# Decoder layer on one core: weight place 4 turned round and filled earlier, last expert tile's rows added in PSUM

## Chip, cores and metric

One NeuronCore of one Trainium2 chip. The metric is the device time of one execution in microseconds (us). Times on the profile's axis count from the first instruction of the profiled execution.

## What is computed

One hybrid decoder layer over 1024 tokens of 1024 float32 values: adaLN modulation, a projection, sparse attention (8 heads) beside differential attention (4 heads), an output projection, then a mixture of experts with 32 experts. The reference, cut to the part that the change touches:

```python
x = x + gate_a[:, None] * jnp.dot(o, w_out[l])
h = rms_norm(x, g_moe[l]) * (1.0 + scale_m[:, None]) + shift_m[:, None]
# hier_moe: top-1 group, top-2 experts in it, gates[token, expert]
y = jnp.zeros_like(h)
for e in range(N_EXPERTS):
    hid = jax.nn.silu(jnp.dot(h, w_gate[e])) * jnp.dot(h, w_up[e])
    y = y + gates[:, e:e + 1] * jnp.dot(hid, w_down[e])
x = x + gate_m[:, None] * y
return rms_norm(x, g_final)
```

## The kernel before

Each engine runs its own list of instructions, written out by hand, and they meet at semaphores. SyncE (SP) issues nearly all plain DMAs, GpSimd (POOL) the indirect ones. Tokens are taken in T = 8 tiles of P = 128.

**Projection loop** (lines 1900 to 1953 on TensorE, 1387 to 1422 on VectorE, 530 to 562 on SyncE). For tile t, TensorE multiplies the attention output in `HT[:, :, 128 t ...]` by `wo` (QKV columns 12288 to 20479, `project_out`, L1861) in two halves of 512 columns; VectorE scales by `gate_row` (QKV columns 22528 to 23551, L1410) and adds the residual into `XT[t]`. The result is stored to DRAM (`residual_rows` for the first 6 tiles, `h_rows` for all 8 normalised ones, `store_h2`), and routing (L1296 and after) chooses experts. It ends with `lst` (L1426), the list of the rows that each expert tile gathers.

**Expert stage.** The pairs of token and expert are packed into NSTEP = 20 expert tiles of 128 rows, numbered 0 to 19. For tile n TensorE runs `turn_rows` (L1963, transposes the gathered rows), `gate_up` (L1976), `turn_hidden` (L1985) and `down_proj` (L1999). ScalarE and VectorE evict between them (ScalarE `ev_t` L950, `ev_sg` L958, `ev_h` L964; VectorE `ev_hid` L1487 and L1489, `ev_y` L1497). POOL gathers the rows of `h_rows` (L690) and scatters each result tile to `expert_rows` in DRAM (`y_dram`, L697). The order on TensorE in a step is

```python
for n in range(NSTEP):
    turn_hidden(n, n % 2)
    if n + 1 < NSTEP: gate_up(n + 1, (n + 1) % 2, *weights_of(n + 1))
    if n + 2 < NSTEP: turn_rows(n + 2, n % 2, 16 * (n // 2 + 2))
    down_proj(n, n % 2, *weights_of(n))
```

**Weights.** An expert has 2 MB of gate and up (`gate_up_load`, L410, two DMAs of 1 MB) and 1 MB of down (`down_load`, L414). The 32 experts pass through RING = 6 places: 0, 1, 3 and 4 are quarters of QKV, 2 lies in X, and place 5 in SC and BIAS. An expert tile takes its rows from one to four experts. SyncE refills a place's gate and up part once the last `gate_up` that needs it is done (`gu_ps`), and its down part after the last `down_proj` (`dn_ps`). Experts 0 to 3 are loaded within or just after the projection loop, gate and up of place 4 after the last `project_out`, and its down part and place 5 only after routing has ended and the first two gathers have landed. `gate_row` lies in place 4's region.

**Tail.** After `down_proj(17)` the 6 spilled residual tiles are read back into `XT` (L572, "x2_back"). When all scatters have landed (`rows_out`), SyncE reads `expert_rows` back, 16 DMAs of 512 KB (L597), two to a token tile. TensorE sums tiles 0, 2, 4 and 6 (`mixed`) in PSUM (`add_into`, L2037): XT times the identity, and each of the two result tiles times a diagonal matrix with its routing weight. VectorE does tiles 1, 3, 5 and 7 (`combine`, L1540 and L1542). ScalarE then squares and sums each tile (L1000), POOL makes the reciprocal root (L635, L636), VectorE scales (`finish`, L1552) and SyncE stores the tile (L600).

## Time and profile before

| | us |
|---|---|
| median of 3 runs | 1051.61 (1050.21 to 1052.73) |
| the profiled execution, its own time | 1047.62 |
| its span, first to last instruction | 1045.8 |
| TensorE busy in the span | 952.2 (91%) |
| VectorE / ScalarE / GpSimd busy | 595.3 / 403.9 / 115.7 |
| mean granted TensorE clock | 0.973 of full |
| DMA: bytes moved | 191.44 MB |

A row's times come from the one profiled execution. "Busy" is the time with an instruction in flight; an idle time is put down to what ended it. The chain of waits goes back from the last instruction to what released each step. The granted clock is 1.00 at 2.4 GHz and 0.50 at 1.2 GHz. In the profile each float32 matmul of 512 columns appears as two records.

### The profile page before, as it was taken

Reading aid. Unit: us, or ns where it says so; the run is one execution under the profiler, and the core shown is the slowest. Engines: PE = TensorE matmul, PEld = TensorE weight load, DVE = VectorE, ACT = ScalarE, POOL = GpSimd, SP = SyncE. Lnnn points to the kernel's source line nnn. Section 1 sums busy time; section 2 is a strip of 40 time slices with the busy share of each in tenths; the row PEclk is TensorE's granted clock in tenths of the full one; section 3 lists DMA queues with packets and bytes.
Section 4 is the critical chain, followed back from the end, with each engine's and each line's share of the span. In section 5 each row is a group of like instructions: output and inputs, shape, how many; then the busy total and the mean of one; then the engine's idle time right before and its main releaser. Section 6 shows DMA issues by size and latency. Waiting matters only on the chain.

```text
span 1045.8 us, 14947 instructions
## 1 busy us (share of the span) xinstructions
PE 952.2 (91%) x5302; PEld 513.1 (49%) x5302; DVE 595.3 (57%) x1593; ACT 403.9 (39%) x909; POOL 115.7 (11%) x218
## 2 busy tenths in 40 slices
PE   3899999999999798879999899999499999979974
PEld 2463675444449476546666545556233434323421
DVE  3479548999997687777676333456333222312217
ACT  6130236666620577767668412122121111211113
POOL 3000000000038001110000000000111111111003
PEclk9999999999999999989999999999599999999989
DMA  9996101101111000040000411166899999999979
GB/s 326 331 359 228 41 22 41 41 21 40 40 30 18 1 1 1 1 173 11 1 2 2 161 61 60 61 261 248 323 418 422 419 417 422 419 421 421 397 284 377
DMA packets 69916, 191.44 MB, mean 183 GB/s; under 512 B 10248, under 2 KB 36160, under 8 KB 57552
## 3 DMA queue, kind: packets, MB, share of 16 engines
q1 hardware_dynamic: 61856, 172.63, 43.1%
q0 software_dynamic: 5760, 16.78, 4.1%
q10 hardware_dynamic: 2224, 1.05, 0.4%
q8 instruction: 43, 0.70, 0.3%
q14 instruction: 33, 0.27, 0.1%
HBM read 172.60 MB, written 22.04 MB: 186 GB/s over the span
## 4 chain that ended last, share of the span: by engine, by line
PE 79%; DMA 6%; issue 4%; DVE 4%; ACT 3%; SPq 3%; POOL 0%; POOLq 0%; ACTq 0%; DVEq 0%
PE PS L1675 16%; PE PS L1976 12%; PE PS L1861 11%; PE PS L1778 6%; PE PS L1999 6%; PE PS L1799 4%; PE PS L1821 3%; DMA SC<-in_w_up_dram 3%; PE PS L1722 3%; PE PS L1684 3%; PE PS L1816 3%; SPq L450 2%; PE PS L1963 2%; PE PS L1699 2%; PE PS L1664 1%
## 5 line engine op out<-in xcount | busy, mean ns | idle before, releaser
L1675 PE MATMUL PS<-HT,X 128*128 128x512 f32 x384 | 168.8, 593 | 0.0
L1976 PE MATMUL PS<-QKV,HT 128*32 128x512 f32 (+2 forms) x640 | 130.4, 607 | 3.4 <-DMA SC<-in_w_up_dram 1.7
L860 ACT ACTIVATE X<-X,nmx 128x896 f32<-128x896 f32 (+7 forms) x128 | 98.6, 772 | 68.5 <-DVE nmx L1205 68.0
L1675 PEld LDWEIGHTS PS<-HT,X 128*128 128x128 f32 x384 | 72.5, 190 | 92.4 <-issue 92.2
L1861 PE MATMUL PS<-QKV,HT 128*128 128x512 f32 x256 | 115.3, 604 | 0.0
L1141 DVE TENSOR_SCALAR_CACHE_REDUCE BIAS<-SC,tk 128x384 f32<-128x384 f32 (+3 forms) x128 | 96.4, 809 | 1.1
L1487 DVE TENSOR_TENSOR HT<-PS,HT 128x256 f32<-128x256 f32 x20 | 8.5, 425 | 153.3 <-ACT HT L958 153.3
L1778 PE MATMUL PS<-QKV 64*128 64x512 f32 (+3 forms) x384 | 82.1, 533 | 10.8 <-DVE nmx L1205 10.0
L837 ACT ACTIVATE X<-SC,tk 128x896 f32<-128x896 f32 x64 | 69.6, 1087 | 43.1 <-DVE tk L1129 43.1
L1861 PEld LDWEIGHTS PS<-QKV,HT 128*128 128x128 f32 x256 | 48.0, 193 | 54.6 <-issue 54.5
L1999 PE MATMUL PS<-QKV,HT 128*32 128x512 f32 (+2 forms) x320 | 65.4, 595 | 2.2 <-DMA X<-in_w_down_dram 2.2
L1205 DVE CUSTOM_DVE_ANT_0 X<-PS,R 128x256 f32<-128x256 f32 (+7 forms) x80 | 51.0, 675 | 28.6 <-PE PS L1778 28.2
L1799 PE MATMUL PS<-ident,X 128*128 128x128 f32 x432 | 66.1, 284 | 0.0
L1976 PE MATMUL PS<-SC,HT 128*32 128x512 f32 (+2 forms) x144 | 57.8, 604 | 6.3 <-issue 6.3
L958 ACT ACTIVATE HT<-PS 128x256 f32<-128x256 f32 x20 | 7.7, 384 | 143.3 <-PE PS L1976 143.3
L1976 PEld LDWEIGHTS PS<-QKV,HT 128*32 128x32 f32 (+2 forms) x640 | 38.1, 120 | 49.0 <-issue 46.2
L1976 PE MATMUL PS<-X,HT 128*32 128x512 f32 (+2 forms) x160 | 58.4, 621 | 0.8 <-DVE HT L1506 0.8
L1205 DVE CUSTOM_DVE_ANT_0 X<-PS,SC 128x1024 f32<-128x1024 f32 (+5 forms) x48 | 42.0, 887 | 29.4 <-PE PS L1778 29.4
L1799 PEld LDWEIGHTS PS<-ident,X 128*128 128x128 f32 x432 | 48.5, 143 | 10.6 <-issue 9.1
L1816 PE MATMUL PS<-QKV,HT 128*128 128x128 f32 x288 | 41.8, 291 | 11.1 <-ACT HT L870 11.0
L1778 PEld LDWEIGHTS PS<-QKV 64*128 64x128 f32 x384 | 32.5, 189 | 39.2 <-issue 25.2
L1821 PE MATMUL PS<-QKV 128*64 128x128 f32 x576 | 46.7, 285 | 4.1 <-ACT QKV L870 2.8
(295 smaller groups left out, 1462.9 us busy)
## 6 DMA issues: line engine op xcount, KB each, us to landing
QKV<-in_w_gate_dram SPq DMA_DIRECT2D x22, 1024.0 KB, 16.4
QKV<-in_w_up_dram SPq DMA_DIRECT2D x22, 1024.0 KB, 22.9
QKV<-in_w_down_dram SPq DMA_DIRECT2D x22, 1024.0 KB, 28.2
QKV<-in_w_ada_dram SPq DMA_DIRECT2D x8, 2048.0 KB, 15.5
QKV<-in_w_ada_dram SPq DMA_DIRECT2D x8, 1024.0 KB, 12.6
X<-in_w_in_dram SPq DMA_DIRECT2D x16, 512.0 KB, 3.8
QKV<-expert_rows SPq DMA_DIRECT2D x16, 512.0 KB, 10.0
X<-in_w_gate_dram SPq DMA_DIRECT2D x5, 1024.0 KB, 16.5
```

The costliest lines, as they stand in the source:

```text
L837: act.activation(RL[:, n % 2, 0:w], SC[:, sc_off[t]:sc_off[t] + w], ACT.Sign, bias=tk[:, 4, i:i + 1].bitcast(F32), scale=-1.0, accum_out=c ...
L860: act.activation(sc, sc, ACT.Exp, bias=nmx[:, i % 4, m:m + 1], scale=-1.0, accum_out=rs[:, i, m:m + 1]).then_inc(exp_done, 1)
L1141: dve.tensor_scalar(BIAS[:, i % 3, 0:w], SC[:, sc_off[t]:sc_off[t] + w], thr.bitcast(F32)[:, i:i + 1], 0.0, ALU.is_lt, ALU.add, accum_out= ...
L1205: dve.tensor_tensor_reduce(sc_buf[i % 4][:, m, 0:w], PS[:, 2 * m:2 * m + 2, :].rearrange("p a n -> p (a n)")[:, BANK * n:BANK * n + w], aw ...
L1675: end = pe.matmul(PS[:, 2 * b + half, :], WS[:, b, j, :], HT[:, j, BANK * half:BANK * (half + 1)], start=(j == 0), stop=(j == KC - 1))
L1778: end = pe.matmul(PS[:, 2 * m + n + c0 // BANK, 0:c1 - c0], QKV[rows_m, q0:q0 + P], QKV[rows_m, k0 + c0:k0 + c1], start=True, stop=True)
L1799: end = pe.transpose(PS[:, 4 + g % 2, c0:c0 + P], sc_buf[i % 4][:, m, P * b:P * (b + 1)], ident[:, :])
L1816: end = pe.matmul(PS[:, 6 + h % 2, slot], turned_at(i)[:, g % 4, P * (b - b0):P * (b - b0 + 1)], vf[:, u * S + P * b:u * S + P * (b + 1)], ...
L1821: end = pe.matmul(PS[DH * m:DH * (m + 1), 6 + h % 2, slot], vd[:, b, v0:v0 + DH], turned_at(i)[:, g % 4, c0:c0 + P], start=(b == 0), stop= ...
L1861: end = pe.matmul(PS[:, n % 4, :], HT[:, k, P * (n // 2):P * (n // 2 + 1)], wo[:, k, BANK * (n % 2):BANK * (n % 2 + 1)], start=(k == 0), s ...
L1976: end = pe.matmul(PS[at, 2 + b, :], hgT[b][:, P * c_ + at.start:P * c_ + at.stop], WGU[w][:, c_, :, :], start=(c_ == 0), stop=(c_ == KC - 1))
L1999: end = pe.matmul(PS[at, 5 + h, :], hidT[b][:, P * c_ + at.start:P * c_ + at.stop], WDN[w][:, c_, BANK * h:BANK * (h + 1)], start=(c_ == 0 ...
```

## The change

1. Place 4 is turned round: its down weights now lie in its first 2048 columns (over `wo`), its gate and up weights in the other 4096 (over `gate_row`). From token tile 4 on, the gate row is read from a second copy, `gate_late`, loaded into the columns of `HT` that `project_out` of tile 0 has used.
2. Gate and up of place 4 are loaded inside the projection loop, at t = 5. Gate and up of place 5 are loaded once all h2 stores have landed and the last router product is done, no longer after the gathers. Its down weights and those of place 4 still come after them.
3. The result tile 19 (LAST) is not scattered. VectorE multiplies it by its rows' routing weights (`w_row`, fetched from DRAM by an indirect DMA at n = 4, `ev_y_last`) and keeps it in `y_last`. A marking matrix `belongs` (128 rows by 1024 tokens, 0 or 1, `mark_last_rows`) says which token each row is of. TensorE adds `belongs` times `y_last` into all 8 token tiles. So that rows nobody scatters read as zero, 32 DMAs write zeros over `expert_rows` during the attention.
4. At the end the order on TensorE is `down_proj(18)` before `gate_up(19)`. The read-back of token tiles 0 to 2 starts once scatter 18 has landed, that of tiles 3 to 7 also waits for `down_proj(19)`.
5. All 8 token tiles are begun in PSUM (`begin`), in two rounds of four pairs of banks; tiles 4 to 7 wait until a pair is free again.

```diff
-        gu_at = [a[:, 0:4096] for a in homes] + [SC[:, 0:4096]]
-        dn_at = [a[:, 4096:6144] for a in homes] + [BIAS[:, 0:2, :].rearrange("p a n -> p (a n)")]
+        gu_at = [a[:, 0:4096] for a in homes[0:4]] + [homes[4][:, 2048:6144], SC[:, 0:4096]]
+        dn_at = [a[:, 4096:6144] for a in homes[0:4]] + [homes[4][:, 0:2048], BIAS[:, 0:2, :].rearrange("p a n -> p (a n)")]
...
+            for r in range(2 * T):
+                for h in range(2):
+                    sp.dma_start(y_dram[P * r:P * (r + 1), BANK * h:BANK * (h + 1)],
+                                 wuk[:, :, :].rearrange("p h d -> p (h d)")).then_inc(small_in, 16)
...
             for t in range(SPILLED):
-                if t == EARLY + 1:
+                if t == 1:
+                    sp.wait_ge(op_ps, 2)
+                    sp.dma_start(gate_late, mod_dram[:, 0:D].partition_broadcast(P).rearrange(
+                        "p o (k n) -> p (o k) n", k=KC)).then_inc(out_row_in, 16)
+                elif t == EARLY + 1:
                     for w in range(IN_X):
                         gate_up_load(sp, expert_of(w), w)
                         down_load(sp, expert_of(w), w)
+                    sp.wait_ge(op_sb, 2 * EARLY)
+                    gate_up_load(sp, expert_of(RING - 2), RING - 2)
...
+            for i in range(2):
+                sp.wait_ge(h2_out[i], 16 * (T // 2))
+            sp.wait_ge(lg_ps, T)
+            gate_up_load(sp, expert_of(RING - 1), RING - 1)
+            sp.wait_ge(route_done, 1)
+            for i in range(2):
+                sp.wait_ge(xg_in[i], 16)
...
             sp.wait_ge(rows_out, 1)
             for t in range(T):
+                if t == 3:
+                    sp.wait_ge(dn_ps, 2 * NSTEP)
                 for k in range(2):
...
+            def ev_y_last():
+                dve.wait_ge(w_in, 16)
+                for h in range(2):
+                    part = slice(BANK * h, BANK * (h + 1))
+                    dve.wait_ge(dn_ps, 2 * LAST + h + 1)
+                    dve.scalar_tensor_tensor(out=y_last[:, part], in0=PS[:, 5 + h, :], scalar=w_row, in1=out_row[:, part],
+                                             op0=ALU.mult, op1=ALU.mult).then_inc(y_sb, 1)
...
+                if n == LAST - 1:
+                    down_proj(n, n % 2, *weights_of(n))
                 if n + 1 < NSTEP:
                     gate_up(n + 1, (n + 1) % 2, *weights_of(n + 1))
                 if n + 2 < NSTEP:
                     turn_rows(n + 2, n % 2, 16 * (n // 2 + 2))
-                down_proj(n, n % 2, *weights_of(n))
+                if n != LAST - 1:
+                    down_proj(n, n % 2, *weights_of(n))
...
+            def begin(t):
+                add_into(t, ident[:, :], XT[:, t, :], True, False)
+                end = add_into(t, belongs[:, P * t:P * (t + 1)], y_last, False, t not in mixed)
+                if t not in mixed:
+                    end.then_inc(mix_ps, 1)
+            def mix(t):
+                i = mixed.index(t)
+                pe.wait_ge(yg_in[t], 32)
+                add_into(t, diag[:, i, 0, :], yg[t][0], False, False)
+                add_into(t, diag[:, i, 1, :], yg[t][1], False, True).then_inc(mix_ps, 1)
             pe.wait_ge(x2_back, 16 * SPILLED)
+            pe.wait_ge(y_sb, 2 * NSTEP)
+            pe.wait_ge(diag_done, 9)
+            pe.wait_ge(rows_out, 1)
+            for t in range(4):
+                begin(t)
+            mix(0)
+            mix(2)
+            pe.wait_ge(fin_done, 1)
+            begin(4)
+            pe.wait_ge(cb_done, 1)
+            begin(5)
+            mix(4)
+            pe.wait_ge(fin_done, 3)
+            begin(6)
+            pe.wait_ge(cb_done, 2)
+            begin(7)
+            mix(6)
```

TensorE at the tail, before (L2037 is the matmul of `add_into`; the rows ahead of it close the branch for overflow tiles):

```order
L2024 REGISTER_ALU
L2024 COMPARE_AND_BRANCH
L2021 UNCONDITIONAL_BRANCH
L2037 MATMUL PS<-X,ident 128x512 x8
L2037 MATMUL PS<-QKV 128x512 x16
L146 UNCONDITIONAL_BRANCH
```

and now, the first twelve groups of four or more (L2112 is the same line of the changed file):

```order
L2112 MATMUL PS<-X,ident 128x512 x2
L2112 MATMUL PS<-QKV 128x512 x2
L2112 MATMUL PS<-X,ident 128x512 x2
L2112 MATMUL PS<-QKV 128x512 x2
L2112 MATMUL PS<-X,ident 128x512 x2
L2112 MATMUL PS<-QKV 128x512 x2
L2112 MATMUL PS<-X,ident 128x512 x2
L2112 MATMUL PS<-QKV 128x512 x10
L2112 MATMUL PS<-X,ident 128x512 x2
L2112 MATMUL PS<-QKV 128x512 x2
L2112 MATMUL PS<-X,ident 128x512 x2
L2112 MATMUL PS<-QKV 128x512 x6
```

Four more groups follow it, of 2, 2, 2 and 6. There were 24 matmuls, there are 48: each of the 8 tiles has two with XT and two with `belongs`, and the mixed ones four more.

TensorE around expert tile 18, before (L1976 `gate_up`, L1999 `down_proj`, L1985 `turn_hidden`):

```order
L1976 MATMUL PS<-SC,HT 32x512
L1976 MATMUL PS<-QKV,HT 32x512 x3
L1999 MATMUL PS<-QKV,HT 128x512 x4
L1985 MATMUL PS<-ident,HT 128x128 x2
L1999 MATMUL PS<-BIAS,HT 32x512
L1999 MATMUL PS<-QKV,HT 32x512 x3
```

and now (L2048, L2071, L2057 are the same three):

```order
L2071 MATMUL PS<-QKV,HT 32x512 x3
L2057 MATMUL PS<-ident,HT 128x128 x2
L2071 MATMUL PS<-QKV,HT 128x512 x4
L2048 MATMUL PS<-SC,HT 32x512
L2048 MATMUL PS<-QKV,HT 32x512 x3
L2048 MATMUL PS<-SC,HT 32x512
```

The four matmuls of `down_proj(18)` stand right behind its own `turn_hidden`, where `gate_up(19)` used to be between them.

SyncE in the projection loop, before, from the loads of place 1 at t = 5 to those of place 2 (L539 stores XT, L522 h2):

```order
L414 DMA QKV<-in_w_down_dram 128x2048
L539 DMA residual_rows<-X 128x1024
L522 DMA h_rows<-SC 128x1024
L527 TENSOR_LOAD eid
L527 ISA x2
L410 ISA
L410 DMA X<-in_w_gate_dram 128x2048
```

and now (L565 and L542 are those stores, L421 a gate and up load):

```order
L425 ISA
L425 DMA QKV<-in_w_down_dram 128x2048
L547 TENSOR_LOAD eid
L547 ISA x2
L421 ISA
L421 DMA QKV<-in_w_gate_dram 128x2048
L421 DMA QKV<-in_w_up_dram 128x2048
L565 DMA residual_rows<-X 128x1024
```

The gate and up load of place 4 now goes ahead of two stores.

## Rows read from the trace of the kernel before

**Rows 1.** The page, 40 slices of the span: GB/s that the DMA engines moved

```profile
GB/s 326 331 359 228 41 22 41 41 21 40 40 30 18 1 1 1 1 173 11 1 2 2 161 61 60 61 261 248 323 418 422 419 417 422 419 421 421 397 284 377
```

**Rows 2.** Waits of TensorE, 888 to 960 us: total us, times, longest us

```profile
PE PS L1976 <- issue: 5.6, 1, 5.6
PE PS L1999 <- DMA X<-in_w_down_dram: 2.2, 1, 2.2
PE PS L1976 <- DMA SC<-in_w_up_dram: 1.7, 1, 1.7
```

**Rows 3.** Chain that ended last, from 988 us: start us, us, what

```profile
988.27 7.07 PE PS L1976 x64
995.34 3.63 PE PS L1999 x8
...
999.23 0.39 ACT HT L964
...
999.67 3.69 PE PS L1999 x32
...
1003.38 0.70 DVE HT L1497
...
1004.85 5.75 DMA expert_rows<-HT,dst_rows
...
1026.68 3.71 PE PS L2037 x8
...
1041.45 1.28 DVE X L1552
```

**Rows 4.** By stretch: PE, PEld, DVE, ACT, POOL busy, granted clock, DMA share, GB/s

```profile
746.97:752.00 5.03, 3.37 (x18) 1.36 (x20) 2.37 (x10) 2.79 (x5) 0.99 (x1) 0.50 0.62 207
752.00:760.00 8.00, 7.93 (x64) 2.56 (x56) 0.52 (x2) 0.41 (x2) 0.00 (x0) 0.89 1.01 409
1003.30:1009.30 6.00, 0.01 (x2) 0.00 (x0) 0.69 (x1) 0.00 (x0) 0.98 (x1) 0.76 0.56 218
```

**Rows 5.** SyncE's DMA issues in order of time: start us, us, line, what

```profile
750.90 0.51 SPq L414 DMA_DIRECT2D BIAS<-in_w_down_dram  x1
759.64 0.34 SPq L410 DMA_DIRECT2D QKV<-in_w_gate_dram  x1
...
987.31 2.98 SPq L572 DMA_DIRECT2D X<-residual_rows  x6
```

**Rows 6.** Down weights issued at 750.90 us: count, KB, us to landing

```profile
BIAS<-in_w_down_dram SPq DMA_DIRECT2D x1, 1024.0 KB, 13.5
```

**Rows 7.** First token gather, issued at 740.29 us: us to landing

```profile
HT<-h_rows,lst POOLq DMA_INDIRECT x1, 5.8
```

**Rows 8.** First expert_rows load, issued at 1010.65 us: us to landing

```profile
QKV<-expert_rows SPq DMA_DIRECT2D x1, 512.0 KB, 3.6
```

**Rows 9.** Tile X, 985 to 1046 us: its DMAs' time to landing

```profile
DMA to landing us min/median/max: 2.6/7.7/19.6
```

**Rows 10.** DMA queues, 1005 to 1006 us: packets, MB, share of 16 engines

```profile
q1 hardware_dynamic: 8, 0.02, 6.1%
```

**Rows 11.** TensorE in order of time, 1009 to 1036 us: start us, us, what

```profile
1009.40 9.03 PE L2037 MATMUL PS<-X,ident 128*128 128x512 f32 x16 [6.09 <-DMA X<-residual_rows]
1018.26 7.03 PE L2037 MATMUL PS<-QKV 128*128 128x512 f32 x16
...
1031.80 3.70 PE L2037 MATMUL PS<-QKV 128*128 128x512 f32 x8 [1.42 <-DMA QKV<-expert_rows]
```

**Rows 12.** VectorE, 996 us on: start us, us, what

```profile
995.81 0.42 DVE L1487 TENSOR_TENSOR HT<-PS,HT 128x256 f32<-128x256 f32 x1 [7.88 <-ACT HT L958]
```

**Rows 13.** The last microseconds in order of time: start us, us, what

```profile
1039.36 1.06 ACT L1000 ACTIVATE HT<-X 128x1024 f32<-128x1024 f32 x1 [2.70 <-DVE X L1542]
...
1040.87 0.54 POOL L636 TENSOR_TENSOR ss<-ss,neghalf 128x1 f32<-128x1 f32 x1
1041.45 1.28 DVE L1552 SCALAR_TENSOR_TENSOR X<-X,ss,BIAS 128x1024 f32<-128x1024 f32 x1 [0.93 <-POOL ss L636]
```

More of the change, by code:

```diff
@@ L266, in hybrid_layer @@
         gate_row, out_row = QKV[:, 22528:22528 + D], R[:, :]
+        gate_late = HT[:, :, 0:P]
         h2 = SC[:, 0:2 * D].rearrange("p (a n) -> p a n", a=2)
@@ L373, in hybrid_layer @@
         diag = QKV[:, 17408:18432].rearrange("p (i k n) -> p i k n", i=4, k=2)
-        yg = [[QKV[:, D * (2 * i + k):D * (2 * i + k + 1)] for k in range(2)] for i in range(T)]
+        yg_at = [18432 + 2 * D * i for i in range(3)] + [2 * D * i for i in range(T - 3)]
+        yg = [[QKV[:, a + D * k:a + D * (k + 1)] for k in range(2)] for a in yg_at]
+        LAST = NSTEP - 1
+        assert last_use[max(range(3, NE, RING))] <= LAST - 2 and last_use[max(range(4, NE, RING))] <= LAST - 1
+        assert max(last_use[w] for w in range(NE - RING)) <= LAST - 2
+        belongs, y_last = QKV[:, 12288:12288 + S], QKV[:, 13312:13312 + D]
+        w_row, d16, tok_last, shift = nmx[:, 0, 0:1], cnt[:, 0, 0:1], cnt[:, 0, 1:2], rs[:, 0:T // 2, :].rearrange("p a b -> p (a b)")
+        w_at, k_tile = (tk[:, i, 0:1].bitcast(I32) for i in range(2))
+        pair_of = lambda t: PS[:, 2 * (t % 4):2 * (t % 4) + 2, :].rearrange("p a n -> p (a n)")
+        mixed_at = {1: 1, 3: 2, 0: 3, 2: 4, 5: 5, 4: 6, 7: 7, 6: 8}
         pick = wuk[:, :, :].rearrange("p h d -> p (h d)").rearrange("p (k t e) -> p k t e", k=2, t=T)
@@ L427, in uses, with scattered @@
             return len(range(b, NSTEP, 2))
+        def scattered(b):
+            return len(range(b, LAST, 2))
         def settle(eng):
@@ L729, in _ @@
                     gather(n + 4)
-                scatter(n)
+                if n < LAST:
+                    scatter(n)
+                if n == 4:
+                    pool.wait_ge(act_in, 48)
+                    pool.indirect_dma_start(out=w_row, out_offset=None, in_=w_dram,
+                                            in_offset=bass.IndirectOffsetOnAxis(ap=w_at.bitcast(U32), axis=0),
+                                            bounds_check=2 * S - 1, oob_is_err=False).then_inc(w_in, 16)
             n_ov = pool.value_load(ovi[0:1, NOV:NOV + 1], min_val=0, max_val=NOV)
@@ L991, in _ @@
                 if t in mixed:
-                    i = mixed.index(t)
-                    act.wait_ge(mix_ps, i + 1)
-                    whole = PS[:, 2 * i:2 * i + 2, :].rearrange("p a n -> p (a n)")
+                    act.wait_ge(mix_ps, mixed_at[t])
+                    whole = pair_of(t)
                 else:
@@ L1489, in ev_hid, with find_last_rows, mark_last_rows @@
                 dve.tensor_tensor(hid[b], hh, PS[:, 2 + b, DE:2 * DE], ALU.mult).then_inc(hid_done, 1)
+            def find_last_rows():
+                link(dve.tensor_scalar(k_tile, dst_rows[:, LAST:NSTEP], 7, None, ALU.arith_shift_right))
+                link(dve.tensor_scalar(d16, dst_rows[:, LAST:NSTEP], 16.0, None, ALU.mult))
+                link(dve.scalar_tensor_tensor(out=w_at, in0=k_tile, scalar=-2047.0, in1=d16, op0=ALU.mult, op1=ALU.add))
+            def mark_last_rows():
+                link(dve.tensor_copy(tok_last, lst[:, LAST:NSTEP]))
+                link(dve.tensor_scalar(shift, first_tok[:, 0:T], tok_last, None, ALU.subtract))
+                for t in range(T):
+                    end = dve.tensor_scalar(belongs[:, P * t:P * (t + 1)], iota_p[:, :], shift[:, t:t + 1], 0.0, ALU.add,
+                                            ALU.is_equal)
+                end.then_inc(diag_done, 1)
+            def ev_y_last():
[5 more added lines that the diff above has]
+                                             op0=ALU.mult, op1=ALU.mult).then_inc(y_sb, 1)
             def ev_y(e, b, stored):
@@ L1508, in ev_t @@
                 end.then_inc(t_sb, 1)
-            dve.wait_ge(modc_set, 1)
+            dve.wait_ge(wgr_ready, 1)
             ev_t(0, 0)
             weigh_experts()
-            dve.wait_ge(out_row_in, 16)
+            dve.wait_ge(out_row_in, 32)
             ev_hid(0, 0)
             ev_t(1, 1)
-            for n in range(NSTEP):
-                if n + 1 < NSTEP:
-                    ev_hid(n + 1, (n + 1) % 2)
-                if n + 2 < NSTEP:
-                    ev_t(n + 2, n % 2)
+            for n in range(LAST - 1):
+                ev_hid(n + 1, (n + 1) % 2)
+                ev_t(n + 2, n % 2)
+                if n == 4:
+                    find_last_rows()
                 ev_y(n, n % 2, n // 2)
+            ev_y(LAST - 1, (LAST - 1) % 2, (LAST - 1) // 2)
+            mark_last_rows()
+            ev_hid(LAST, LAST % 2)
+            ev_y_last()
             dve.wait_ge(route_done, 2)
```

91 lines of the change are left out of this document (44 added, 47 removed).

## The prediction

> **What bounds the kernel now.** I read the page's slices first. From slice 30 (about 758 us) to slice 37 the DMA engines move 397 to 423 GB/s without a dip [rows 1], so I take the expert stage to be weight traffic with TensorE just behind it. The waits of TensorE say how far behind: between 888 and 960 us it stands still for 5.6, 2.2 and 1.7 us, 9.5 us in all, twice by name for weights [rows 2]. The 5.6 us are put down to "issue"; I read them as the third weight wait, since nothing else in that step is new. Then I read the chain from 988 us: `gate_up(19)`, `down_proj(18)`, `down_proj(19)`, the eviction at 1003.38, the last scatter of 5.75 us, and after it the read-back of `expert_rows` [rows 3]. Last, TensorE's own list: it starts the tail at 1009.40, works 16 records in 9.03 us and 16 more in 7.03, and then waits for rows between groups of 8 records of 3.70 us each [rows 11]. So before the change the tail is fed by data and TensorE has slack in it.
>
> **Earlier weights (parts 1 and 2).** Gate and up of place 4 leave the queue at 730 us; those of place 5, 2.1 MB, move from after 749 us to about 734 us. The second is what counts behind routing. The amount gained is not 2.1 MB / 0.42 = 5 us by itself, since refills wait for TensorE, and an engine that has run dry gets nothing back. Between 747 and 751 us 1.05 MB (down 4), 3.15 MB (place 5), 0.5 MB (gate row for the results) and a gather of 0.5 MB are issued, 5.2 MB; until 760 us 5.03 us x 207 GB/s + 8 us x 409 GB/s = 4.3 MB have moved [rows 4]. About 0.9 MB or 2.2 us of backlog is left when SyncE issues the first refill at 759.64 [rows 5]. That is the mean engine. But a load lands with its slowest engine, and the down load issued at 750.90 took 13.5 us, to 764.4 [rows 5, 6], 4.8 us after that refill. The gain lies between 2.2 and 4.8 us; I take 4, as each matmul waits for whole loads.
>
> The trace has a sign of such an engine: at 1005 us the queue of the plain loads keeps 6.1% of the 16 engines busy, which is one engine of 16, on 8 packets [rows 10]. The Trainium skill's DMA: Bandwidth & Descriptors (Latency and other measured facts) says that engines 7 and 15 are usually slower than the others in traces. By an even spread the gain would be 2.2 us, by that rule 4.8. The trace's tail agrees that one lags, though it doesn't give its number.
>
> The first gather took 5.8 us with weights of place 4 in the queue [rows 7]. Now place 5's are, issued a little later but behind less. A load of the same size into an empty queue took 3.6 us [rows 8]. So the gain is between 0 and 2.2 us; I take 1, the middle, since 2.1 MB are in flight in either case. Together **5 us earlier** at the end of the expert stage (0 to 9.5, since TensorE can't win more than it waited, and 2.2 for the gather on top).
>
> The zero stores (8.4 MB) run in the attention, where the page shows 1 to 40 GB/s in most slices [rows 1]; nothing waits. If it weren't so, 20 us of traffic would delay `wo`. The earlier load at t = 5 pushes the last stores of the loop back by 5 us, into a stretch of low traffic before routing. `gate_late` is one load of 512 KB with a tile's time to land. `mark_last_rows` and `find_last_rows` are 13 small VectorE instructions in a stretch in which it idles 7.88 us at a time [rows 12]. These I cost at nothing.
>
> **The order at the end (part 4).** On the old axis `turn_hidden(18)` ends at 987.6. ScalarE's eviction (0.39) is no longer covered, then `down_proj(18)` 3.63 and `gate_up(19)` 7.07 [rows 3], to 998.7. Now nothing covers the activation (0.39), the two multiplications (0.42 each), `turn_hidden` (0.4) and its eviction (0.39): to about 1001. `down_proj(19)` 3.69 and VectorE's last half 0.70 [rows 3] give `y_last` at 1005.4, against 1004.08 before, so 1.3 us later. Less the 5 us: **1000.4**. What it buys: scatter 18 lands about 6 us earlier and scatter 19 (5.75 us [rows 3]) is gone, so SyncE starts to read back at about 1000 instead of 1010.65.
>
> **What the tail then waits for.** TensorE also waits for the six residual tiles. They are issued from 987.31 on [rows 5], the last lands 19.6 us after its issue [rows 9], which is the 1009.40 at which TensorE starts today [rows 11]. This is DMA work in a line, so it comes earlier by the same 5 us: 1004.4. That is later than 1000.4 and decides: **S = 1004.4** (lower bound: a gain of 11.5 us in both, 997.9; upper: no gain, 1009.4).
>
> **TensorE's tail (parts 3 and 5).** 48 matmuls in place of 24. Sixteen records, which are eight matmuls, take 7.03 us less the overlap of the last one; the loads of the array behind them stand 0.43 us apart, so a matmul costs 0.86 us [rows 11] and 48 cost **41.3 us**, where 24 cost 20.6. They are in one row of dependences, and the data for them is there: with a start at 1000 the read-back of 8.4 MB is done by about 1022 at some 410 GB/s, while `mix(6)` comes 38 us after S. VectorE has 4 x 2.56 + 8 x 1.28 = 20.5 us of work beside it, ScalarE 10. The wait for `finish(0)` ahead of `begin(4)` adds some **0.3**: square 1.1, root 0.8, scaling 1.28 [rows 13] against `mix(2)`'s 3.4. The clock: TensorE idles 6 us before the tail today, the granted clock falls to a mean of 0.76 in it [rows 4], and the first 16 records take 9.03 us and not 7.03 [rows 11]. In the changed kernel it idles from 999.7 to 1004.4, so I take the same **2.0** (0 if the wait is short). Behind `mix(6)` come square 6 and 7 (1.1 each), the root (0.8), the scaling (1.28) and the last store (1045.8 - 1042.73 = 3.1), with gaps **7.7 us** [rows 13].
>
> **Sum.** 1004.4 + 2.0 + 41.3 + 0.3 + 7.7 = 1055.7 against a span of 1045.8: **+9.9 us**. In other words the stretch from TensorE's first tail matmul to the end grows from 36.4 to 51.3 us, and 5 us come back ahead of it. The profiled execution took 1047.62, so the changed one should take about 1057.5; it lay 4 us below the median of the runs, 1051.61, so the median should be about **1061.5**.
>
> **Rivals.**
> - *The tail stays fed by data (faster).* Today TensorE waits 1.42 us for rows ahead of its last group [rows 11], and the read-back starts some 10 us earlier. If it still set the end, all behind it would come about 9.6 us earlier: near 1042. That needs the added matmuls to hide. With S = 1004.4 and 10 us around them, 48 matmuls may take 31.7 us for no change, 0.66 us each; below that the change wins. The row says 0.86 [rows 11], so I give it **6%**, mostly for a mistake of mine in S.
> - *All stalls come back and S is early (no change).* With the full 11.5 us, S = 997.9 and no fall of the clock: 1047.3, +1.5 us, 1053. It needs the DMA engines never to run dry after 747 us, against the 0.9 MB of backlog at 760 [rows 4]. **8%**, half of it within the bound of the measurement.
> - *The early load gives nothing, or the read-back delays the residual tiles (slower still).* SyncE now issues the first six read-backs at about 1000 us, when the residual tiles are still on the way. S stays at 1009.4 or goes past it: 1009.4 + 51.3 = 1060.7, +15 us, 1066.5. The last residual tile hangs on one engine [rows 10], which speaks for it; that the plain loads share a queue and keep their order speaks against. **14%**.
>
> **Numbers.** The forecast holds 72%, with a range of its own of 1057 to 1065. The whole range takes in most of the second and third rival: 1053 to 1067. A measurement of this kernel tells 0.2%, 2.1 us, from no change. Faster 6%, the same 4%, slower 90%.
>
> **What would show it.** Right: 96 records at the line of `add_into`, spaced 0.43 us and with hardly a gap, from about 1004 us on; TensorE's own idle time at the tail named after the residual tiles; read-back rows landed well ahead of `mix`; the three weight waits of 9.5 us cut to about 5; DMA below 400 GB/s for a few us before 760. Wrong: TensorE waiting for `expert_rows` in the tail, records closer than 0.43 us, or a start of the tail before 998 us.

## The result, and the profile after

| | before | the change |
|---|---|---|
| median of the runs beside each other | 1050.95 us (6 runs) | 1065.14 us (6 runs) |
| profiled execution, its span | 1047.62, 1045.8 us | 1065.57, 1063.8 us |
| first `gate_up` starts | 749.8 | 755.0 |
| last record of `down_proj` starts | 1002.7 | 1012.8 |
| first matmul of the tail (S) | 1009.4 | 1014.4 |
| from S to the end | 36.4 | 49.4 |

The change makes the kernel slower: 1.0137 times before, 95% interval 1.0115 to 1.0158, which is 14.2 us. (Of the runs further below, one of E4's ten took 1445.88 us at a mean granted clock of 0.65 and stands outside its ratio.) The two spans differ by 18.0 us, and that has to be split before it is read. 3.8 us of it lie ahead of 82 us, in the start-up, which the change doesn't touch: the first projection matmul starts at 77.9 before and at 81.7 after, and in the twelve profiles further below anywhere between 77.9 and 81.6, whichever edit they carry. Another 1.4 us lie between that matmul and the first of `project_out`. In the twelve profiles this stretch differs from before by -1.3 (E5) to +2.3 us (E11), and not with the zero stores: with them E3 has 0.0, without them E1 has 0.0 and E1d +1.5. From here on, times inside the expert stage are counted **from the first `gate_up`**, which takes this spread out.

TensorE's waits between 893 and 1020 us, which answer to [rows 2] (total us, times, longest us):

```profile
PE PS L2048 <- issue: 5.8, 1, 5.8
PE PS L2071 <- issue: 2.7, 1, 2.7
PE PS L2071 <- DMA X<-in_w_down_dram: 1.6, 1, 1.6
PE PS L2048 <- DMA SC<-in_w_up_dram: 1.5, 1, 1.5
PE PS L2057 <- DVE HT L1533: 1.4, 1, 1.4
PE PS L2112 <- DVE QKV L1556: 0.9, 1, 0.9
PE PS L2071 <- ACT HT L1000: 0.5, 1, 0.5
```

The three weight waits are still there, 5.8 + 1.6 + 1.5 = 8.9 us against 9.5, and a new one of 2.7 us stands at `down_proj` (L2071). The first tail matmul (L2112) waits 0.9 us for `y_last` (L1556), not for a residual tile.

The chain that ended last, from 988 us (start us, us, what), against [rows 3]:

```profile
988.61 3.57 PE PS L2071 x32
...
993.04 2.30 issue
995.34 5.05 PE PS L2071 x8
1000.40 7.05 PE PS L2048 x64
...
1007.88 0.44 DVE HT L1531
...
1009.80 3.69 PE PS L2071 x32
...
1013.51 0.76 DVE QKV L1556
...
1014.36 20.84 PE PS L2112 x48
...
1035.22 20.88 PE PS L2112 x48
1056.13 1.12 ACT HT L1037 x2
```

The scatter that stood in this chain before is gone from it, and so is every wait for data. In its place are 96 TensorE records in two blocks without a gap: 20.84 and 20.88 us for 48 records each, 0.434 us a record and 0.87 a matmul. Ahead of them `down_proj(18)` takes 5.05 us for the work of 3.63, because the clock fell (by stretch: us, busy times of PE, PEld, DVE, ACT and POOL, granted clock, DMA share, GB/s):

```profile
995.30:997.00 1.70, 1.66 (x2) 0.84 (x3) 0.00 (x0) 0.00 (x0) 0.00 (x0) 0.50 1.01 402
...
1014.30:1016.00 1.70, 1.64 (x4) 0.87 (x5) 0.00 (x0) 0.00 (x0) 0.00 (x0) 1.00 1.01 325
```

After its wait of 2.7 us TensorE is granted half of its clock, 1.2 GHz, and is late by 1.4 us when it gets through. What it waits for is the down weights of its expert. The trace says "issue", but where it records the landing of that load (in E5, E6 and E11 further below), the first matmul follows it by 0.09 us each time. In E6 the load is issued at 960.29 us and the matmul starts at 989.91; between them lie (count, KB, us to landing)

```profile
QKV<-in_w_down_dram SPq DMA_DIRECT2D x1, 1024.0 KB, 29.5
```

At the start of the tail TensorE had stood for 0.9 us, and the granted clock is 1.00, where before it stood for 6.09 and had a mean of 0.76 [rows 4, 11].

What became of the earlier weights shows in the DMA rate around the first refill. Two of SyncE's issues after (start us, us, what), then the stretches behind the first `gate_up` at 755.0:

```profile
754.20 0.34 SPq L425 DMA_DIRECT2D BIAS<-in_w_down_dram  x1
764.93 0.34 SPq L421 DMA_DIRECT2D QKV<-in_w_gate_dram  x1
```

```profile
755.00:763.00 8.00, 7.99 (x56) 2.08 (x60) 0.88 (x5) 1.26 (x1) 0.12 (x1) 0.74 0.83 324
763.00:765.00 2.00, 2.00 (x20) 1.05 (x12) 0.26 (x1) 0.38 (x1) 0.00 (x0) 1.00 0.11 45
765.00:767.00 2.00, 0.78 (x9) 0.40 (x11) 1.86 (x6) 1.73 (x5) 0.99 (x1) 1.00 0.56 102
767.00:775.00 8.00, 8.00 (x72) 2.90 (x72) 0.46 (x2) 0.43 (x2) 0.00 (x0) 1.00 1.01 420
```

and the same stretches of the kernel before, from its first `gate_up` at 749.8:

```profile
749.80:757.80 8.00, 8.00 (x56) 2.05 (x60) 0.85 (x5) 1.24 (x1) 0.09 (x1) 0.75 0.97 370
757.80:759.80 2.00, 2.00 (x20) 1.09 (x12) 0.36 (x1) 0.39 (x1) 0.00 (x0) 1.00 1.02 420
759.80:761.80 2.00, 0.78 (x8) 0.46 (x10) 1.77 (x6) 1.78 (x5) 0.99 (x1) 1.00 1.01 426
```

At the first `gate_up` the changed kernel is ahead by 2.18 MB. Then its DMA engines run dry: 370 - 324 GB/s over 8 us, 420 - 45 over 2 and 426 - 102 over 2 make 0.37 + 0.75 + 0.65 = 1.77 MB handed back by 12 us, 0.41 MB or 1 us left. By 30 us after the first `gate_up`, 0.09 MB is left. The refill can't be issued before TensorE frees a place, 9.9 us after the first `gate_up` in both kernels (764.93 - 755.0; 759.64 - 749.8 = 9.8 in [rows 5]).

### The profile page after: what moved, and what is told of

The parts are those of the page before. It is cut to its first block, busy times and chain, and to the rows that moved or that the text cites. A ratio compares the mean times of both kernels' runs of the same rounds, so it can differ in the third digit from the quotient of the medians.

```text
span 1063.8 us, 15097 instructions
## 1 busy us (share of the span) xinstructions
PE 977.4 (92%) x5350; PEld 525.0 (49%) x5350; DVE 597.9 (56%) x1606; ACT 404.2 (38%) x909; POOL 113.3 (11%) x219
## 4 chain that ended last, share of the span: by engine, by line
PE 83%; issue 5%; DMA 4%; DVE 4%; ACT 3%; POOL 0%; SPq 0%; DVEq 0%; ACTq 0%; POOLq 0%
PE PS L1747 16%; PE PS L2048 12%; PE PS L1933 11%; PE PS L2071 6%; PE PS L1850 6%; PE PS L1871 4%; PE PS L2112 4%; PE PS L1893 3%; PE PS L1794 3%; DMA SC<-in_w_up_dram 3%; PE PS L1756 3%; PE PS L1888 2%; PE PS L2035 2%; PE PS L1771 2%; PE PS L1712 1%
## 5 line engine op out<-in xcount | busy, mean ns | idle before, releaser
L2048 PE MATMUL PS<-QKV,HT 128*32 128x512 f32 (+2 forms) x640 | 130.9, 609 | 3.1 <-ACT HT L986 1.7
L1850 PE MATMUL PS<-QKV 64*128 64x512 f32 (+3 forms) x384 | 81.6, 530 | 11.6 <-DVE nmx L1242 10.8
L2071 PE MATMUL PS<-QKV,HT 128*32 128x512 f32 (+2 forms) x320 | 66.8, 600 | 4.3 <-issue 2.7
L2048 PE MATMUL PS<-SC,HT 128*32 128x512 f32 (+2 forms) x144 | 58.2, 607 | 5.8 <-issue 5.8
L2048 PEld LDWEIGHTS PS<-QKV,HT 128*32 128x32 f32 (+2 forms) x640 | 38.2, 120 | 48.8 <-issue 46.0
L2048 PE MATMUL PS<-X,HT 128*32 128x512 f32 (+2 forms) x160 | 58.5, 622 | 0.8 <-DVE HT L1574 0.8
L1242 DVE CUSTOM_DVE_ANT_0 X<-PS,SC 128x1024 f32<-128x1024 f32 (+5 forms) x48 | 42.0, 887 | 27.6 <-PE PS L1850 27.6
## 6 DMA issues: line engine op xcount, KB each, us to landing
QKV<-in_w_ada_dram SPq DMA_DIRECT2D x8, 1024.0 KB, 12.8
QKV<-expert_rows SPq DMA_DIRECT2D x16, 512.0 KB, 11.3
```

Of the source, the lines that this page charges most:

```text
L1242: dve.tensor_tensor_reduce(sc_buf[i % 4][:, m, 0:w], PS[:, 2 * m:2 * m + 2, :].rearrange("p a n -> p (a n)")[:, BANK * n:BANK * n + w], aw ...
L1850: end = pe.matmul(PS[:, 2 * m + n + c0 // BANK, 0:c1 - c0], QKV[rows_m, q0:q0 + P], QKV[rows_m, k0 + c0:k0 + c1], start=True, stop=True)
L2048: end = pe.matmul(PS[at, 2 + b, :], hgT[b][:, P * c_ + at.start:P * c_ + at.stop], WGU[w][:, c_, :, :], start=(c_ == 0), stop=(c_ == KC - 1))
L2071: end = pe.matmul(PS[at, 5 + h, :], hidT[b][:, P * c_ + at.start:P * c_ + at.stop], WDN[w][:, c_, BANK * h:BANK * (h + 1)], start=(c_ == 0 ...
```

## The experiments

All were run beside the kernel before on the same chip; ratios are to it, with their 95% interval. Before's median was 1050.7 us beside E1 to E4, 1051.9 beside E1d, E5, E6 and E8, 1051.7 beside E7, E9 and E10, and 1049.9 beside E11.

### The parts alone: E1 to E4

**E1** is before with the weight part alone (place 4 turned round, gate and up of places 4 and 5 moved forward):

```
+                    sp.wait_ge(op_sb, 2 * EARLY)
+                    gate_up_load(sp, expert_of(RING - 2), RING - 2)
...
+            sp.wait_ge(lg_ps, T)
+            gate_up_load(sp, expert_of(RING - 1), RING - 1)
+            sp.wait_ge(route_done, 1)
```

> The kernel before with the weight part alone: place 4 turned round, its gate and up loaded at t = 5, those of place 5 before the gathers, the late gate row. Theory A (the lead is given back because the refills wait for TensorE and the queue runs dry about 8 to 12 us after gate_up(0)): the time stays within 2 us of before, the DMA rate shows a hole of some 4 us right after the first expert tile starts, and the weight waits of TensorE between tiles 13 and 15 stay at 8 to 10 us. Rival B (each weight comes from the slowest DMA engine, which never runs dry): 3 to 5 us faster, and these waits shrink to about 5 us. Rival C (the weight part costs something in the projection loop): 1 to 4 us slower with TensorE idle ahead of the routing.

Measured: 1051.56 us, ratio 1.000 (0.998 to 1.002). The weight part is worth nothing, as theory A said. Its DMA rate has the same hole (10 and 119 GB/s where before has 420 and 426), its three weight waits are 8.9 us, and its last `down_proj` starts 252.3 us after its first `gate_up`, against 252.9 before. Its profile loses 2.8 us between the first `project_out` and the first `gate_up`; the change, with the same loads, takes 159.6 us for this stretch as before does, so this isn't the price of the loads.

**E2** is the changed kernel with before's weight loads, so the tail part alone.

> The changed kernel with its weight loads as before: only the last tile's handling, the new order at expert tile 18 and the zero stores remain. Theory A (all of the loss is in the tail and the order, the weight part is worth nothing): 12 to 16 us slower than before, equal to the changed kernel within 2 us. Rival B (the weight part hides some of the loss): 16 to 20 us slower. If the zero stores cost anything, TensorE's list between 400 and 480 us is longer by 1 to 2 us than before.

Measured: 1068.58 us, ratio 1.0158 (1.0133 to 1.0184), 3.4 us more than the change; the intervals still overlap. It is 17.9 us over before, outside theory A's 12 to 16 and within rival B's 16 to 20. Its chain shows where (start us, us, what):

```profile
992.93 2.44 issue
995.37 6.62 PE PS L2058 x8
...
1011.39 5.34 PE PS L2058 x32
```

Both last `down_proj` run at the lowered clock for a while, 6.62 and 5.34 us, where the change paid 5.05 and 3.69: 3.2 us. Whether that belongs to the weight loads is taken up by E10.

**E3** is the changed kernel with `down_proj(18)` behind `gate_up(19)` again, as before (VectorE's eviction of its results moves back with it, which the cut leaves out):

```
-                if n == LAST - 1:
-                    down_proj(n, n % 2, *weights_of(n))
...
-                if n != LAST - 1:
-                    down_proj(n, n % 2, *weights_of(n))
+                down_proj(n, n % 2, *weights_of(n))
```

> The changed kernel with down_proj(18) behind gate_up(19) again. Theory A (moving it forward makes TensorE wait for down weights that land when they always did, some 2.3 us of wait and 1.4 us of slower clock, and uncovers 1.3 us of evictions): y_last is ready 4 to 5 us earlier; the tail can start only when the residual tiles are back and scatter 18 has landed, which were 5 and 2 us later than the old y_last, so of these 4 to 5 us only 0 to 3 reach the end. Rival B (the order is needed for the read-back): slower by 2 to 6 us, with TensorE waiting for expert_rows in the tail.

Measured: 1062.22 us, ratio 1.0114 (1.0091 to 1.0137), 2.9 us less than the change, whose interval begins at 1.0115, so that the two are hardly told apart. The last `down_proj` starts 252.9 us after the first `gate_up`, as before, and not 257.8. But now the tail waits for the scatter of tile 18:

```profile
1001.95 9.01 DMA expert_rows<-HT,dst_rows
...
1011.17 23.01 PE PS L2109 x48
```

TensorE stands for 6.4 us, its clock falls, and 48 records take 23.01 us where the change needs 20.84. Counted from the first `gate_up`, the tail starts at 259.9 us here and at 259.4 in the change, and the execution ends at 311.5 against 308.8. So the new order costs 4.9 us at the last `down_proj`, and nothing at the start of the tail, because the old one would have waited there for the scatter. The two measures don't agree on the end: by the medians E3 is 2.9 us shorter than the change, by the profiles from the first `gate_up` on it is 2.7 us longer, and E10 repeats the change at a ratio of 1.0117, next to E3's 1.0114. Whether the order costs anything in all is not shown.

**E4** is the changed kernel without the 16 matmuls by `belongs`. It leaves out the results of the last expert tile.

```
-                end = add_into(t, belongs[:, P * t:P * (t + 1)], y_last, False, t not in mixed)
```

> The changed kernel without the 16 matmuls that multiply y_last by the marking matrix; the results of expert tile 19 are left out of the output. Theory A (TensorE's 48 matmuls of 0.86 us in a row set the tail): 13 to 14 us faster than the changed kernel, that is about the time of before, and TensorE's first to last record of the tail takes 28 to 31 us in place of 41.7. Rival B (the tail is set by the read-back or by VectorE): less than 8 us faster, and TensorE waits for rows or for VectorE in the tail.

Measured: 1050.90 us, ratio 1.0009 (0.9986 to 1.0032). Sixteen matmuls less take off 14.2 us, which is 0.89 for each and the whole loss. TensorE's two tail blocks shrink as they should, from 20.84 and 20.88 us:

```profile
1013.42 13.97 PE PS L2112 x32
1027.39 0.03 issue
1027.41 14.02 PE PS L2112 x32
```

This kernel has no last scatter and no marking either, and is still only level with before. From its first tail matmul to the end it takes 35.7 us, before 36.4: the 32 matmuls that are left take 28.0 and what lies behind them 7.7, so that TensorE binds this tail too, and the read-back, though earlier, sets nothing.

### How early is too early: E1d

E1 with the down weight of place 4 also loaded before the first gathers:

```
+            down_load(sp, expert_of(RING - 2), RING - 2)
             gate_up_load(sp, expert_of(RING - 1), RING - 1)
```

> E1 (the weight part alone, 1051.6 us) with the down weight of place 4 also loaded before the first gathers, so one megabyte more (2.5 us at the 409 GB/s of [rows 4]) lies ahead of them. Theory A (the lead that a place loaded early gives is handed back in the DMA hole of 8 to 12 us after the first gate_up, because the refills wait for a place to come free): no change, 1050 to 1053 us. Rival B (the early place works through the slowest DMA engine, and E1 had too little of it): 2 to 3 us less than E1, about 1049. Rival C (what lies ahead of the gathers delays them by its own transfer time): 2 us more than E1, about 1053.5, with the first gate_up later by as much.

Measured: 1053.76 us, ratio 1.0023 (1.0001 to 1.0044). That is rival C's number, 2.2 us over E1, though the two intervals overlap. The profile has the delay in the gathers (start us, us, what; then the median us to landing; then TensorE's wait):

```profile
745.42 1.31 POOL L698 DMA_INDIRECT HT<-h_rows,lst  x1 [12.42 <-DVE lst L1440]
```

```profile
HT<-h_rows,lst POOLq DMA_INDIRECT x2, 9.1
```

```profile
PE PS L1977 <- DMA HT<-h_rows,lst: 10.6, 1, 10.6
```

9.1 us to landing where before has 5.8 [rows 7], and a wait of 10.6 us where TensorE waits 7.0 before and 6.9 in E1. From the last matmul of `project_out` to the first `gate_up` it takes 29.6 us, against 26.1 before and 27.6 in E1. The slowest-engine reading, by which one more early megabyte should have been worth 2 to 3 us, has no support.

### What the marking costs, and what it has to cost: E5 to E7

**E5**: the marking matrix in bf16, and `y_last` as the sum of two bf16 halves.

```
+                    link(dve.tensor_copy(y_hi[:, part], y_last[:, part]))
+                    dve.tensor_tensor(y_lo[:, part], y_last[:, part], y_hi[:, part], ALU.subtract).then_inc(y_sb, 1)
...
+                add_into(t, belongs[:, P * t:P * (t + 1)], y_hi, False, False)
+                end = add_into(t, belongs[:, P * t:P * (t + 1)], y_lo, False, t not in mixed)
```

> The changed kernel with the marking matrix in bf16 and the last tile's rows split into a bf16 part and a bf16 rest: 32 single-pass matmuls of about 0.22 us instead of 16 float32 ones of 0.86 us, so 7.0 us of TensorE work instead of 13.8, against four more VectorE operations (about 2 us) ahead of the first tail matmul. Theory A (the tail is bound by TensorE, and E4's 14.2 us are the matmuls themselves): 1065.1 - 6.8 + 2 = 1060.3 us, 1058.5 to 1062. Rival B (the cost of the marking lies in what it waits for, not in its matmuls): 1065 to 1067. The tail's first matmul to the end: 42.5 us by A, 49 by B.

Measured: 1059.07 us, ratio 1.0080 (1.0050 to 1.0111): 6.1 us less than the change, and 34.3 us from its first to its last tail record. By TensorE's groups (line, operation, names, shapes, count | busy us, mean ns | idle before):

```profile
L2116 PE MATMUL PS<-X,ident 128*128 128x512 f32 x32 | 15.2, 598 | 2.4 <-DVE QKV L1561 2.3
L2116 PE MATMUL PS<-QKV 128*128 128x512 f32 x32 | 14.2, 592 | 0.0
L2116 PE MATMUL PS<-QKV 128*128 128x512 bf16 x30 | 7.9, 379 | 0.1
```

The f32 matmuls have two records each (16 matmuls, x32), the bf16 ones a single one (30 of the 32 are in the trace): two bf16 matmuls cost 0.5 us where one f32 costs 0.87.

**E6**: the odd tiles' residual is added by VectorE, in one more pass per tile; their identity matmuls are gone.

```
+                if t in mixed:
+                    add_into(t, ident[:, :], XT[:, t, :], True, False)
...
+                dve.wait_ge(mix_ps, mixed_at[t])
+                dve.tensor_tensor(XT[:, t, :], XT[:, t, :], pair_of(t), ALU.add).then_inc(cb_done, 1)
```

> The changed kernel with the odd tiles' residual added by VectorE (one more pass of about 1.2 us for each of four tiles) instead of by two identity matmuls each: 8 float32 matmuls, 6.9 us, leave TensorE. Theory A (TensorE bound, VectorE has room): 1065.1 - 6.9 = 1058.2 us, 1057 to 1060. Rival B (VectorE's added passes stand in front of combine and finish and hold the banks that TensorE waits for): 1061 to 1064, with TensorE idle at the tail for DVE.

Measured: 1058.68 us, ratio 1.0088 (1.0055 to 1.0121), 6.5 us less than the change. Eight matmuls fewer, and two blocks of 40 records that still have no gap:

```profile
1007.54 17.41 PE PS L2113 x40
1024.95 0.03 issue
1024.98 17.45 PE PS L2113 x40
```

**E7** has both edits, E5's and E6's.

> The changed kernel with both savings, the bf16 marking of E5 and the odd tiles' residual on VectorE of E6. They took 6.1 and 6.5 us off 1065.1 one by one. Theory A (both come off TensorE's chain, and it still binds the tail): 1065.1 - 12.6 = 1052.5 us. Rival B (VectorE's three passes for each odd tile bind the tail, as E8's chain showed, with 9 of its last 25 us in them): 1054 to 1057.

Measured: 1053.87 us, ratio 1.0033 (1.0008 to 1.0057). 11.3 us less than the change, where the parts gave 12.5 (6.07 + 6.46). Theory A's 1052.5 lies at the very end of the interval, rival B's low end within it. The time alone doesn't tell the two apart; the trace does. TensorE has its work done without a pause, but behind its last matmul stand 9.7 us and not 7.7, and VectorE is busy for 19.57 us of the 19.80 before the last scaling (columns as above):

```profile
1027.10:1046.90 19.80, 15.34 (x44) 6.30 (x42) 19.57 (x16) 7.08 (x14) 5.95 (x12) 0.94 0.55 222
```

That is rival B's mechanism, at a price of some 2 us.

### In search of a version that wins: E8, E9, E11

**E8** puts E7's tail on E3's order, with TensorE's wait for the scatters behind the first two tiles.

> A version meant to beat both: E3's order (down_proj of tile 18 behind gate_up of tile 19), the marking in bf16 of E5, the odd tiles' residual on VectorE of E6, and the first tiles' matmuls no longer behind the wait for the scatters. TensorE's tail then holds 8 identity matmuls (6.9 us), 32 bf16 ones (7.0) and 16 of the diagonals (13.8): 27.7 us against 20.6 before and 41.3 in the change. Theory A (the tail is then bound by the data once more: the scatter of tile 18, the read-back, the stores): as E4's without its 5 us in the order of the end, but the scatter of tile 18 ends as late as in E3; 1048 to 1051 us, no better than before by more than 3. Rival B (TensorE still binds): 1053 to 1056. In the trace A shows TensorE idle for the tiles' rows several times in the tail, B shows it in one piece.

Measured: 1055.07 us, ratio 1.0035 (1.0015 to 1.0056), where A had 1048 to 1051. The number is rival B's (1053 to 1056), and so is its sign: but for 0.2 us TensorE doesn't stand still after its first tail matmul. But the chain names two things that neither had:

```profile
993.74 19.28 DMA X<-residual_rows
...
1028.16 1.29 DVE X L1629
1029.44 1.20 DVE X L1616
...
1030.67 1.31 DVE X L1618
...
1032.01 1.22 DVE X L1621
1033.22 2.39 DVE X L1629 x2
```

The last residual tile takes 19.28 us to land, at 1013.02, which is 259.7 us after the first `gate_up`; before it is 259.6 [rows 9, 11]. And behind it VectorE, with three passes for an odd tile, works without a pause from 1028.16 us to 1047.9, and once more for the last tile.

**E9** keeps the change's order and E5's marking, and adds the marks to the odd tiles' residual while VectorE waits for the first rows of the read-back:

```
+            for t in (1, 3, 5, 7):
+                dve.wait_ge(mix_ps, mixed_at[t])
+                dve.tensor_tensor(XT[:, t, :], XT[:, t, :], pair_of(t), ALU.add).then_inc(cb_done, 1)
             combine(1)
```

> E7 written so that nothing is added where VectorE is busy: TensorE marks the odd tiles first, VectorE adds that to their residual while it waits for the first rows of the read-back (12.7 us of idle time in E8), so combine keeps its two passes, and the identity matmuls of tile 0 stand ahead of the wait for the last rows. The order of tiles 18 and 19 is the changed kernel's, whose read-back begins 254.5 us after the first gate_up, against 259.6 before. Theory A (the earlier read-back is worth having once TensorE has little to do): TensorE's tail is 28.6 us of work, of which 1.7 lies ahead of the last rows; from 257.8 + 2.6 us after the first gate_up that ends at 289, the last square, rstd, finish and store at 297, against 296.0 before: 1049 to 1052 us, level with before, because TensorE's chain and the data's now end together. Rival B (a real gain, the data's chain alone counts: 254.5 + 36.4 = 291): 1046 to 1048. Rival C (marks and adds in turn make TensorE wait for VectorE at the start): 1053 to 1056.

Measured: 1053.02 us, ratio 1.0024 (0.9999 to 1.0049). That is above theory A's 1049 to 1052 and at the low end of rival C; but TensorE waits for VectorE for only 0.8 us in its tail. In its chain two costs stand out, the slow `down_proj(18)` and a load of one vector:

```profile
989.86 6.64 PE PS L2078 x8
...
1006.39 9.05 DMA BIAS<-in_g_final_dram
```

**E11** is E9 with that vector loaded in the middle of the expert stage:

```
+                if n == 10:
+                    act.dma_start(gfin, g_final.partition_broadcast(P)).then_inc(act_in, 16)
```

> E9 with the load of g_final issued by ScalarE in the middle of the expert stage (tile 10) instead of behind it. In E9's chain this load (issued 1006.39, landed 1015.45) held VectorE's first added pass, and with it TensorE's marks of tiles 5 and 7 and all that follows, where the last tile's rows were ready at 1011.2. Theory A (that wait is on the path): the first pass starts about 3 us earlier, 1053.0 - 3 = 1050 us, 1048.5 to 1051, level with before or a little faster. Rival B (E9's tail waits for the rows of the read-back anyway): 1052 to 1053.5.

Measured: 1050.60 us, ratio 1.0012 (0.9987 to 1.0037). The load is gone from the chain, the ratio falls by 1.2 thousandths (the intervals overlap, so that a gain isn't shown), and the last residual tile decides again (issued at 992.58, landed at 1009.83). This is the best version with the last tile's results added on chip, and it is no faster than the kernel before.

### The change once more: E10

> The changed kernel itself once more, for its spread: theory A (E2's 3.4 us more than the change are the slower clock at down_proj of tiles 18 and 19 that its profile showed, a matter of the order at the end and not of the weights) expects 1065 to 1069 us here, with the time from the first gate_up to the last down_proj between 257 and 262. Rival B (E2's loads of place 4 are worse than the change's by themselves): 1065 within 0.7.

Measured: 1063.25 us, ratio 1.0117 (1.0083 to 1.0152), and 258.9 us from the first `gate_up` to the last `down_proj`. The stretch is as A said and the time is not.

```profile
990.18 2.00 issue
992.18 5.35 PE PS L2071 x8
...
1006.93 3.68 PE PS L2071 x32
```

`down_proj(18)` is slow again, `down_proj(19)` is not, as in the change's first profile. E4 has the change's weight loads and pays 6.51 and 5.33, as E2 does with before's. So the second slow `down_proj` doesn't go with the weight loads. What calls it forth stays open, and with it why the number is that of E2's rival B, and whether E2's 3.4 us over the change (5.3 over this run) have any other part. Rival B's point, 1065 within 0.7, is missed as well: two series of one kernel stand 1.9 us apart.

## Why the prediction came out as it did

The forecast was 1061.5 us and slower, with 1057 to 1065 as its own range and 1053 to 1067 as the whole one; the two series of the change gave 1065.1 and 1063.3. So the time lies at the upper end of its own range, and part of the nearness is luck: a gain of 5 us that didn't come and a loss of 2 us that wasn't paid stand against each other. The mechanism, a tail in which TensorE's float32 matmuls take the place of a wait for data, is right. Of the terms around it, two of the sum were wrong with opposite signs, and two that don't enter it were wrong as well.

- **The matmuls: right.** 0.86 us each and 41.3 us in all were forecast from [rows 11]; the two blocks take 20.84 + 20.88 = 41.7 us, the 0.3 us for the wait ahead of `begin(4)` among them. E4, E5 and E6 take the price apart from three sides: 14.2 us for 16, 6.5 us for 8, 6.1 us for the marking in bf16. The 7.7 us behind `mix(6)` are 1063.8 - 1056.11 = 7.7.
- **The clock in the tail: wrong, +2.0 forecast, 0 measured.** The forecast had TensorE idle from 999.7 to 1004.4; it idled for 0.9 us and kept a granted clock of 1.00. It was right for the case it described: E3 idles 6.4 us, and its first 48 records take 2.2 us more. The clock was lost elsewhere, at `down_proj(18)`, 1.4 us in the change's profile and 1.5 to 3.0 in E5, E10, E4, E7, E2 and E9, which the forecast did not have.
- **Earlier weights: wrong, -5 forecast, about 0 measured.** This is the largest miss. I chose 4 us, near the load that lands with its slowest engine, over the 2.2 us of mean backlog, and even 2.2 was too much. The step that failed is the price by backlog: it took what the DMA engines have in advance at 760 us to stay an advance. They emptied 8 us after the first `gate_up`, and the next refill has to wait until TensorE frees a place, 9.9 us after it; nothing of what was loaded early moves that. The upper price, 4.8 us, which the Trainium skill's DMA: Bandwidth & Descriptors (Latency and other measured facts) supported with its slower engines 7 and 15 (for a cause that it guesses at and calls specific to the software queue, whereas SyncE's loads go by the hardware one [rows 10]), falls with it: E1 and E1d show no such gain. They don't show that all engines are alike. The 1 us for the gather is not there either: the first one lands after 5.72 us against 5.76 (5.1 to 6.6 us in the other profiles with the change's loads), and E1d shows the other sign, 9.1 us with one more megabyte ahead.
- **The order at the end: mis-sized, +1.3 forecast for `y_last`, +5.0 measured.** Counted from the first `gate_up`, `y_last` is ready at 1014.27 - 755.0 = 259.3, and the last half of the results before at 1004.08 - 749.8 = 254.3. The uncovered evictions are there as worked out. What was left out is that `down_proj(18)` comes forward to a moment at which TensorE first stands 2.7 us and then takes 1.4 us longer at a lower clock. In the nine profiles with this order (the change, E2, E4 to E7, E9 to E11) it starts 240.0 to 241.5 us after the first `gate_up`, whatever was done elsewhere. It waits there for its weights, which land in E6 240.1 us after the first `gate_up`; before they land at 240.8, but `down_proj(18)` starts only at 245.5, so that nobody waits. E3 shows the term as a whole, 4.9 us, and also that it is not felt at the start of the tail.
- **What sets S: wrong name.** The prediction let the last residual tile decide, at 1004.4. `y_last` decided, at 1014.27, and TensorE waited for VectorE. But three things end together there, counted from the first `gate_up`: `y_last` in the change at 259.3, the scatter of tile 18 in E3 at 259.6, and the last residual tile at 257.7 in E6 (989.0 + 18.4 - 749.7), 259.0 in E11, 259.7 in E8 and 259.6 before. To take away one of them moves S little. It was 259.6 before and is 259.4 now; the forecast of -5 falls with the lead of the weights, which the residual tiles, queued behind the same traffic, would have had to inherit. What did come earlier is the read-back, from 260.9 (1010.65) to 254.5 us (1009.53), and no one waited for it.
- **Sum.** From S to the end +13.0 us (14.9 forecast, 2.0 of them the clock), in front of S from the first `gate_up` on -0.2 (-5.0 forecast): +12.8 us where +9.9 was forecast, and +14.2 and +11.6 in the two series.
- **The rivals.** The tail fed by data would have needed 0.66 us a matmul, and it took 0.87. (The prediction's own figures, 1045.8 - 1004.4 - 10 = 31.4 us, give 0.65; and its 11.5 us of stalls are 9.5 + 2.2 = 11.7.) E7 brings TensorE's tail down to 28.0 us, 0.58 for each of 48, and is still slower, 1.0033 (1.0008 to 1.0057), because that reckoning put S 5.0 us ahead of where it was before, and in E7 it lies 4.3 behind (263.9 us after the first `gate_up`, against 259.6), with VectorE's 2 us on top. The full gain of all stalls failed with the lead. The third, S back at its old place and 1066.5 us, had 14%, and its first half is what happened: E1 shows that the early load gives nothing. Of its second half, the read-back that delays the residual tiles, nothing was seen: the last residual tile lands at 259.7 in E8 and 259.6 before, where the read-back starts after it, and at 257.7 in E6 and 259.0 in E11, where it is issued some 5 us before that. It deserved far more, since the prediction itself says that the refills wait for TensorE.

Of the signs listed, the 96 records without a gap, the read-back well ahead of `mix` (no tail wait but the 0.9 us), and the dip of the DMA rate came true; the dip, at 763 us or 757.8 on the axis of before, was where it should be, but it was the failure of the gain, not a mark of it. The start from about 1004, the residual tiles' name on the wait and the cut of the weight waits to about 5 us did not.

## What to carry to other kernels

A round trip through memory that costs nobody anything should be priced against what replaces it on the engine that is busiest there: here a scatter and a wait of 6 us gave way to 13.8 us of float32 matmuls, and a bf16 marking matrix with the rows split in two would have cost about half. A head start in a ring of buffers is worth nothing when the next refill is tied to a buffer coming free; look for when that happens, not at how many bytes are ahead. And an instruction group that is moved forward arrives at what it needs, data and clock, earlier too: ask whether they are there.

## What the runs showed of the hardware that was not expected

- The granted clock of TensorE fell to 0.50, 1.2 GHz, behind 2.7 us of idling at `down_proj(18)` in the change (5.05 us for 3.63 us of work), and E10's 5.35 us behind 2.4 look the same. In E6 3.1 us of idling were followed by 3.67 us at a granted clock of 1.00, and in E11 1.7 us. Kernels with the same instructions there differ by up to 3 us in this. E6's profile is of the shortest of its five runs (1052.57 us, mean granted clock 0.977, median 1058.68), so it need not be usual for it.
- The time of an execution of one kernel goes with its mean granted clock: beside E7, E9 and E10 the kernel before took 1047.0 to 1047.5 us in the four runs at 0.973, and 1052.0 to 1054.8 in the five at 0.964.
- A scatter of 128 rows by index took 5.75 us before [rows 3], beside 154 GB/s of traffic in all, and 9.01 us in E3, beside 196; they ended 260.8 and 259.6 us after the first `gate_up`. That the traffic is the cause isn't shown.
- A load of one vector of 1024 numbers, spread over all 128 partitions (512 KB), took 9.05 us to land in E9 between the residual tiles and the read-back, and 8.4 us in E11 in the middle of the expert stage.
- The start-up ahead of the first projection matmul differs by up to 3.8 us between single profiled executions (77.9 to 81.7 us), the change and its own repetition among them (81.7 and 78.1). A difference of spans should be cut at such a point before it is explained.
